# A two-layer hybrid decoder trunk: identity products on TensorE in front of nine of its waits

## The chip, the core and the metric

The kernel runs on one core of one Trainium2 chip. Each run gives one time, the device microseconds from launch to end. The profile is one execution of its own, with a span from the first to the last instruction. TensorE is called PE in the profile; its weight loads are a lane of their own (PEld), VectorE is DVE, ScalarE is ACT, GpSimd is POOL and SyncE is SP.

## The reference

Input x is 512 tokens by 1024 features, float32. Two layers, each with two residual steps, and a last norm:

```
for layer in (0, 1):
    hn = rms_norm(h, norm_mix_g[layer])
    proj = hn @ w_in[layer]                 # 1024 -> 2560, ten slices of 256
    y = concat(rg_lru(...)*gelu, hgrn2(...), multiscale_pool(...), sb*conv(sc*sx))
    h = h + y @ w_out[layer]                # 1024 -> 1024
    hn = rms_norm(h, norm_ffn_g[layer])
    if layer == 0: h = h + (silu(hn @ w_gate) * (hn @ w_up)) @ w_down        # 2816 wide
    else:          h = h + moe_swiglu(hn, w_router, w1, w3, w2)              # top 2 of 8, 3584 wide
out = rms_norm(h, final_norm_g)
```

The hgrn2 mixer is a gated linear recurrence, computed in chunks; the router takes two experts a token, and an expert computes `(silu(x @ w1[e]) * (x @ w3[e])) @ w2[e]` for its tokens.

## The kernel before

All engines run from hand-written queues: each engine's program is a list of instructions in the order of the code, and semaphores (`wait_ge`, `then_inc`) hold them apart. There is no scheduler; TensorE does what stands next in its list or waits for it.

**Precision.** Most matrix products are written as three fp32r products, `mm3` (lines 567 to 570): every operand is split into a high part and a rest, and hi*hi, hi*lo and lo*hi are added in PSUM. The splitting of weights is ScalarE's (`w_hi`) and VectorE's (`w_lo`) work. A second sort of product is plain float32: the levels of the hgrn2 scores (L629), the gates (L639), the pool product (L646), state updates (L688, L699, L704), the fold of the router's logits (L785), the rank counts (L789 to L793) and the picking of token rows (L968). A third sort is the transpose by the identity tile `idt`, also float32 (L586, L677, L717, L819, L854). `idt` is a 128x128 float32 tile that is loaded once.

**Stages on TensorE.** Per layer: `norm_transposes(2*layer)` turns four row tiles of 128 tokens (8 transposes each) into PSUM banks; ten `project` calls, with `level` calls between them; `hgrn_tail(layer)`, which does the output projection in pieces as the mixers' results arrive; `norm_transposes(2*layer+1)`; then in layer 0 a loop of 11 dense chunks, and in layer 1 the router and a loop over expert items. Norms are numbered m = 0 to 3 in that order.

**The norms.** ScalarE squares a row tile and sums it, VectorE and ScalarE make the scale, VectorE writes the scaled row (L1314), and TensorE transposes it (L586). For norms 0 to 2 the rows go alternately to two buffers, `ex_63` and `ex_64`, so VectorE may write row 2 only when TensorE has transposed row 0, and row 3 only after row 1 (`if i >= 2 and m < 3: dve.wait_ge(tr_done, 4 * m + i - 1)` in `norm_row`, L1313). Norm 3 has four buffers and no such wait. After the fourth row ScalarE and VectorE copy the banks out (L1020, L1329), and the next products start. In norms 1 and 3 the transposes of row 0 into banks 4 to 7 also wait for `h_ready`: these banks hold the output projection until VectorE has added it to h (L1612).

**End of the input projection.** After level 7 (L629) TensorE waits at the head of `hgrn_tail` for `pl_read`, `y_lo` and `w_lo_done`: VectorE must have split the first two mixers' results (L1412). `sb_read` is counted up by VectorE where it reads the slice SB out of PSUM (L1521), some instructions before.

**Router.** `mm3` with the router's weights into bank 0; VectorE copies the logits (`logits_copied`), TensorE folds them (L785), VectorE computes the two best experts (`route_ready`), TensorE counts ranks (L789 to L793), VectorE makes a 0/1 matrix `pick` (`pick_ready`), TensorE multiplies the token rows with it (L968), which gives the first item's tokens turned; VectorE and ScalarE split them into `xt` (L1173, L1709, L1714), and the first expert products (L898, L900) wait for that, and for `items_ready`.

Of the kernel before, what the change touches and what calls it, by code (L numbers as in the profile page):

```python
# [29 lines left out]
P = 128  # L30
# [69 lines left out]
def build(nc, x, w_in, w_out, w_gate, w_up, w_down, w_router, w1, w3, w2, norm_rows, params, ident,  # L100
          masks, moe_const, zeros, out):
    ctx = ExitStack()
    with ctx:
# [11 lines left out]
        def sb(name, shape, dt=F32):  # L115
            t = at(name, shape, dt, base[0])
            base[0] += size(shape, dt)
            return t

        def sem(name):  # L120
            return ctx.enter_context(nc.semaphore(name))
# [6 lines left out]
        idt = sb("idt", [P, P])  # L128
# [38 lines left out]
        def rows_of(m, i):  # L167

            return rows[i if m == 3 else i % 2]
# [54 lines left out]
        ps = ctx.enter_context(nc.psum_tensor("ps", [P, 8, 512], F32))  # L224
# [34 lines left out]
        sb_read = sem("sb_read")  # L259
# [306 lines left out]
        def _(pe):  # L566
# [8 lines left out]
            def wlo(n, k=KT):  # L575
                return w_los[:, n % 3, :].rearrange("p (k n) -> p k n", k=k)

            def norm_transposes(m):
                for i in range(NT):
                    pe.wait_ge(rows_done, 4 * m + i + 1)  # L580
                    for k in range(KT):
                        if i == 0 and k >= 4 and m % 2:
                            pe.wait_ge(h_ready, 4 * (m // 2) + k - 3)
                        if i == 0 and k in (4, 6) and m == 2:
                            pe.wait_ge(down_added, 4 * DC + k // 2 + 1)
                        last = pe.transpose(ps[:, k, i * P:(i + 1) * P], rows_of(m, i)[:, k * P:(k + 1) * P],  # L586
                                            idt[:, :])
                    last.then_inc(tr_done, 1)
# [77 lines left out]

            def hgrn_tail(layer):
                first = layer * LAYER1 + N_IN
                pe.wait_ge(pl_read, 2 * (layer + 1))
                pe.wait_ge(y_lo, 4 * layer + 2)  # L670
                pe.wait_ge(w_lo_done, first + 1)
# [13 lines left out]
                for c in range(NT - 1):  # L685
                    for hd in range(NH):
# [3 lines left out]
                                         start=True, stop=True)  # L690
                last.then_inc(ds_done, 1)
                pool_product(layer, 0)
                for c in range(NT):
# [4 lines left out]
                    for hd in range(NH):  # L698
                        last = pe.matmul(o_of(hd, c), scores[:, hd, c, :], vals[:, c, hd * HD:(hd + 1) * HD],  # L699
                                         start=c == 0 and hd < 2, stop=False)  # L700
                    if c:
                        for hd in range(NH):
# [3 lines left out]
                                             stop=c == NT - 1 and hd >= 2)  # L706
# [55 lines left out]
            for layer in range(DEPTH):  # L762
                norm_transposes(2 * layer)
                for i in range(N_IN):
                    project(layer, i)
                    if i >= 2:
                        level(layer, i - 2)
                    if i == 5:
                        gates(layer)
                hgrn_tail(layer)  # L770
                norm_transposes(2 * layer + 1)
                if layer == 0:
                    with pe.Fori(0, DC) as c:
                        dense_chunk(c)
# [3 lines left out]
            for k in range(KT):  # L778
                pe.wait_ge(in_lo, 3 * KT + k + 1)
                last = mm3(ps[0:NE, 0, :], wr_hi[:, k, :], wr_lo[:, k, :], act_hi[:, k, :], act_lo[:, k, :],  # L780
                           k == 0, k == KT - 1)
            last.then_inc(logits_turned, 1)
            pe.wait_ge(logits_copied, 1)
            for tt in range(NT):
                last = pe.matmul(ps[:, 1, tt * NE:(tt + 1) * NE], fold[0:NE, tt * P:(tt + 1) * P],  # L785
                                 idt[0:NE, 0:NE], start=True, stop=True)
            last.then_inc(logits_done, 1)
            pe.wait_ge(route_ready, 1)
            pe.matmul(ps[:, 3, 0:NT * NE], mcon[:, MC_LOWER:MC_LOWER + P], rt[:, 8, :], start=True, stop=False)  # L789
            for j in range(1, NT):  # L790
                last = pe.matmul(ps[:, 3, j * NE:NT * NE], mcon[:, MC_ONES:MC_ONES + P], rt[:, 8, 0:(NT - j) * NE],
                                 start=False, stop=j == NT - 1)
# [131 lines left out]
            def item_turned(n):  # L924
# [37 lines left out]
                    last.then_inc(yt_tr, 1)  # L962
                pe.sem_inc(t_done, 2 * EC)

            pe.wait_ge(pick_ready, 1)
            for k in range(KT):
                for i in range(NT):
# [2 lines left out]
                if k in (5, KT - 1):  # L970
                    last.then_inc(xt_tr, 1)

            turned_next = pe.alloc_register("pe_turned_next")
            pe.wait_ge(items_ready, 1)
            n_items = pe.value_load(items[0:1, 32:33], min_val=2, max_val=MAX_ITEMS)
# [304 lines left out]
        def _(dve):  # L1280
# [109 lines left out]
            def level_operand(layer, lv):  # L1390
                half = 1 << (lv - 1)
                if lv >= 3:
                    dve.wait_ge(level_done, 4 * (layer * LEVELS + lv - 1))
                dve.wait_ge(exp_done, 7 * layer + lv)
                e_left, e_right = views(ex[lv % 2], half)
                x_left, x_right = views(xs[lv % 2], half)
                k_left, _ = views(keys, half)
                _, q_right = views(qf, half)
                dve.tensor_tensor(x_left, k_left, e_left, ALU.mult)
                dve.tensor_tensor(x_right, q_right, e_right, ALU.mult).then_inc(xs_ready, 1)  # L1400
# [641 lines left out]
```

## Time and profile before

| | |
|---|---|
| time, three runs | 2129.79 us median (2128.96 to 2131.98) |
| the profiled execution | 2134.22 us, of which the span 2132.6 us |
| PE busy | 2012.5 us, 94% of the span |
| PEld / DVE / ACT / POOL busy | 84% / 73% / 52% / 5% |
| chain that ended last | PE 78%, DVE 11%, ACT 5%, issue 5% |
| mean granted TensorE clock | 0.976 of full speed |

How to read it: the granted clock has two levels here, 1.00 (2.4 GHz) and 0.50 (1.2 GHz), and the mean of a window says how much of it was spent at either. A matmul's time in the timeline is from its start to a modelled end; matmuls overlap, so the pace is read from a run of them: (time of the run less one matmul) by (count less one), or window by count. In a timeline row "[7.00 <-issue]" is the time that the engine stood idle before the row and what ended it; "issue" is a wait whose releaser the profile doesn't name. The start of a merged row is that of its first instruction; x32 is the number of instructions in it.

### The profile page before, as it was taken

The numbers are of one execution on the slowest core, as the hardware profiler recorded it, in microseconds if no ns is written. First come the engines' busy times: TensorE is split into PE (matmuls) and PEld (weight loads), VectorE is DVE, ScalarE is ACT, GpSimd is POOL, SyncE is SP. The second block draws the span as 40 slices with busy tenths as digits, with TensorE's granted clock in tenths as the row PEclk, the third lists the DMA queues.
The fourth block names the chain that finished last, engine by engine and source line by source line (L and its number), as shares of the span: only waits on it lengthen the run. The fifth ranks groups of instructions, "written<-read, shape, count | busy, mean of one in ns | idle before, by whom it ended". The sixth has DMA issues, their size and how long they took to land.

```text
span 2132.6 us, 33531 instructions
## 1 busy us (share of the span) xinstructions
PE 2012.5 (94%) x12158; PEld 1782.0 (84%) x12159; DVE 1549.3 (73%) x1622; ACT 1109.5 (52%) x1272; POOL 113.1 (5%) x105
## 2 busy tenths in 40 slices
PE   7998999999989988899999999999999999999993
PEld 6777878778778777899999988788999888999782
DVE  6766553443557484788878889899788898888896
ACT  5532433233335423455555577777555776555773
POOL 0000000000000000300010020200100201000202
PEclk9999999999999999899999999999999999999997
DMA  5311732323322121777677789999777899777983
GB/s 189 104 55 50 257 100 78 118 77 100 98 79 79 60 69 67 245 256 256 234 256 258 258 304 378 345 379 359 264 252 257 301 374 332 245 246 258 352 329 140
DMA packets 218795, 450.95 MB, mean 211 GB/s; under 512 B 13073, under 2 KB 64289, under 8 KB 218753
## 3 DMA queue, kind: packets, MB, share of 16 engines
q1 hardware_dynamic: 210256, 420.53, 56.7%
q0 software_dynamic: 8496, 29.85, 3.8%
q8 instruction: 28, 0.46, 0.1%
q14 instruction: 15, 0.11, 0.0%
HBM read 432.50 MB, written 17.84 MB: 211 GB/s over the span
## 4 chain that ended last, share of the span: by engine, by line
PE 78%; DVE 11%; ACT 5%; issue 5%; DMA 1%; POOL 0%; DVEq 0%; ACTq 0%; SPq 0%; POOLq 0%
PE ps L568 16%; PE ps L570 16%; PE ps L569 16%; PE ps L898 12%; PE ps L915 8%; PE ps L900 5%; PE ps L917 3%; DVE w_lo L1703 2%; DVE w_lo L1291 1%; ACT w_hi L998 1%; ACT w_hi L1149 1%; ACT w_hi L1151 1%; PE ps L629 1%; DMA raw<-in_w_in_dram 1%; DVE scores L1408 1%
## 5 line engine op out<-in xcount | busy, mean ns | idle before, releaser
L1703 DVE TENSOR_TENSOR w_lo<-raw,w_hi 128x2048 fp32r<-128x2048 f32 x340 | 768.7, 2285 | 136.5 <-ACT w_hi L1151 134.3
L898 PE MATMUL ps<-xt,w_hi 128*128 128x320 f32 x1792 | 465.3, 347 | 3.9 <-DVE xt L1714 3.6
L900 PE MATMUL ps<-xt,w_lo 128*128 128x160 f32 x1792 | 424.2, 237 | 0.0
L1149 ACT ACTIVATE w_hi<-raw 128x1024 fp32r<-128x1024 f32 x340 | 357.3, 1051 | 118.9 <-PE ps L900 62.1
L1151 ACT ACTIVATE w_hi<-raw 128x1024 fp32r<-128x1024 f32 x340 | 356.3, 1048 | 0.0
L900 PEld LDWEIGHTS ps<-xt,w_lo 128*128 128x128 f32 x1792 | 343.1, 191 | 0.1
L898 PEld LDWEIGHTS ps<-xt,w_hi 128*128 128x128 f32 x1792 | 337.2, 188 | 4.5 <-issue 4.4
L568 PE MATMUL ps<-act_hi,w_hi 128*128 128x512 f32 x608 | 244.3, 402 | 14.4 <-DVE act_lo L1329 7.2
L915 PE MATMUL ps<-ht,w_hi 128*128 128x320 f32 x896 | 235.9, 348 | 8.5 <-DVE gated L1823 8.5
L569 PE MATMUL ps<-act_lo,w_hi 128*128 128x512 f32 x608 | 242.5, 399 | 0.0
L570 PE MATMUL ps<-act_hi,w_lo 128*128 128x512 f32 x608 | 242.2, 398 | 0.0
L917 PE MATMUL ps<-ht,w_lo 128*128 128x160 f32 x896 | 212.1, 237 | 0.0
L568 PE MATMUL ps<-w_hi,xt 128*128 128x512 f32 x448 | 177.6, 397 | 0.7 <-issue 0.7
L570 PE MATMUL ps<-w_hi,xt 128*128 128x512 f32 x448 | 178.0, 397 | 0.0
L569 PE MATMUL ps<-w_lo,xt 128*128 128x512 f32 x448 | 177.1, 395 | 0.0
L915 PEld LDWEIGHTS ps<-ht,w_hi 128*128 128x128 f32 x896 | 168.1, 188 | 10.7 <-DVE gated L1823 5.7
L917 PEld LDWEIGHTS ps<-ht,w_lo 128*128 128x128 f32 x896 | 171.1, 191 | 0.0
L568 PEld LDWEIGHTS ps<-act_hi,w_hi 128*128 128x128 f32 x608 | 116.2, 191 | 44.8 <-issue 12.3
L1638 DVE TENSOR_TENSOR hid_d<-silu_d,ps 128x512 f32<-128x512 f32 x22 | 15.1, 688 | 172.3 <-PE ps L570 172.3
L570 PEld LDWEIGHTS ps<-act_hi,w_lo 128*128 128x128 f32 x608 | 116.1, 191 | 27.5
L569 PEld LDWEIGHTS ps<-act_lo,w_hi 128*128 128x128 f32 x608 | 116.2, 191 | 26.7
L568 PE MATMUL ps<-w_hi,act_hi 128*128 128x256 f32 x384 | 112.4, 293 | 18.4 <-issue 14.0
(322 smaller groups left out, 3104.8 us busy)
## 6 DMA issues: line engine op xcount, KB each, us to landing
raw<-in_moe_w_dram SPq DMA_DIRECT2D x672, 512.0 KB, 5.1
raw<-in_w_in_dram SPq DMA_DIRECT2D x20, 1024.0 KB, 5.1
raw<-in_ffn_w_gate_dram SPq DMA_DIRECT2D x11, 1024.0 KB, 5.4
raw<-in_ffn_w_up_dram SPq DMA_DIRECT2D x11, 1024.0 KB, 5.4
raw<-in_ffn_w_down_dram SPq DMA_DIRECT2D x11, 1024.0 KB, 4.8
raw<-in_w_out_dram SPq DMA_DIRECT2D x8, 1024.0 KB, 4.9
y_rows<-mult POOLq DMA_DIRECT2D x1, 8192.0 KB, 25.6
y_rows<-yacc POOLq DMA_DIRECT2D x8, 512.0 KB, 5.2
```

The costliest lines, as they stand in the source:

```text
L568: pe.matmul(o_, lhi, rhi, start=start, stop=False)
L569: pe.matmul(o_, lhi, rlo, start=False, stop=False)
L570: return pe.matmul(o_, llo, rhi, start=False, stop=stop)
L629: last = pe.matmul(ps[:, 4 + 2 * ct + half, c * P:(c + 1) * P], a, b, start=True, stop=True)
L898: pe.matmul(pairs_of(ps[:, bank, 0:2 * NW]), hi_[:, k % 4, f * P:(f + 1) * P], xt[:, k, :, 0:NW], start=k == 0, stop=False)
L900: last = pe.matmul(ps[:, bank, NW:2 * NW], lo_[:, k % 4, f * P:(f + 1) * P], xt[:, k, 0, 0:NW], start=False, stop=k == KT - 1)
L915: pe.matmul(pairs_of(ps[:, bank, 0:2 * NW]), hi_[:, f % 2, d * P:(d + 1) * P], ht_n[:, f, :, :], start=f == 0, stop=False)
L917: last = pe.matmul(ps[:, bank, NW:2 * NW], lo_[:, f % 2, d * P:(d + 1) * P], ht_n[:, f, 0, :], start=False, stop=f == 3)
L998: act.activation(w_his[:, n % 3, :], raw[:, n % 3, :], ACT.Copy).then_inc(w_hi_done, 1)
L1149: act.activation(slot_hi[p % 6][:, 0:half], raw6(p)[:, 0:half], ACT.Copy)
L1151: act.activation(slot_hi[p % 6][:, half:PIECE], raw6(p)[:, half:PIECE], ACT.Copy).then_inc(w_hi_done, 1)
L1703: dve.tensor_tensor(slot_lo[p % 6], raw6(p), f32(slot_hi[p % 6]), ALU.subtract) \
```

## The change

A helper `spin(o_, n)` issues n products of the identity tile with itself, float32, 128x128 by 128x128, into a part of PSUM that nothing reads. It is called with fixed counts at seven places of the code, which nine times run in a launch:

| place | count | stands in front of |
|---|---|---|
| head of `hgrn_tail`, both layers | 55, 55 | `pl_read`, `y_lo`, `w_lo_done` |
| norms 1 and 3, row 0, before k = 6 | 26, 26 | `h_ready` |
| norm 2, before row 0 | 28 | `rows_done` |
| after the router's logits | 6 | `logits_copied` |
| after the fold | 26 | `route_ready` |
| after the rank counts | 14 | `pick_ready` |
| after the picking | 28 | `items_ready`, then `xt_lo_done` |

That is 264 products. In `hgrn_tail` a wait for `sb_read` is new as well, since bank 0 holds a slice that VectorE reads. No other line is changed.

```
+            def spin(o_, n):
+                for _ in range(n):
+                    pe.matmul(o_, idt[:, :], idt[:, :], start=True, stop=True)
+
             def norm_transposes(m):
                 for i in range(NT):
+                    if m == 2 and i == 0:
+                        spin(ps[:, 0, 0:P], 28)
                     pe.wait_ge(rows_done, 4 * m + i + 1)
                     for k in range(KT):
+                        if i == 0 and k == 6 and m % 2:
+                            spin(ps[:, 0, P:2 * P], 26)
...
             def hgrn_tail(layer):
                 first = layer * LAYER1 + N_IN
+                pe.wait_ge(sb_read, 2 * (layer + 1))
+                spin(ps[:, 0, 0:P], 55)
                 pe.wait_ge(pl_read, 2 * (layer + 1))
                 pe.wait_ge(y_lo, 4 * layer + 2)
...
             last.then_inc(logits_turned, 1)
+            spin(ps[:, 7, 0:P], 6)
             pe.wait_ge(logits_copied, 1)
...
             last.then_inc(logits_done, 1)
+            spin(ps[:, 7, 0:P], 26)
             pe.wait_ge(route_ready, 1)
...
+            spin(ps[:, 7, 0:P], 14)
             pe.wait_ge(pick_ready, 1)
...
+            spin(ps[:, 7, 0:P], 28)
             turned_next = pe.alloc_register("pe_turned_next")
             pe.wait_ge(items_ready, 1)
```

The order of TensorE's list at the head of `hgrn_tail` in layer 0, before (L629 is the last level, L568 to L570 the output projection; the brackets name the semaphores waited for):

```order
L570 MATMUL ps<-act_hi,w_lo 128x512
L629 MATMUL ps<-xs_66 128x128 [waits level_read,xs_ready]
L629 MATMUL ps<-xs_66 128x128 x7
L629 MATMUL ps<-xs_66 128x128 [waits level_read]
L629 MATMUL ps<-xs_66 128x128 x7
L568 MATMUL ps<-w_hi,act_hi 128x256 [waits w_lo_done,y_lo,pl_read]
```

The same place now (the line numbers are those of the changed file; L637 is L629 of before, L580 the identity product):

```order
L637 MATMUL ps<-xs_66 128x128 [waits level_read,xs_ready]
L637 MATMUL ps<-xs_66 128x128 x7
L637 MATMUL ps<-xs_66 128x128 [waits level_read]
L637 MATMUL ps<-xs_66 128x128 x7
L580 MATMUL ps<-idt 128x128 [waits sb_read]
L580 MATMUL ps<-idt 128x128 x54
L568 MATMUL ps<-w_hi,act_hi 128x256 [waits w_lo_done,y_lo,pl_read]
```

The 55 products stand between the last level and the wait that the output projection had; nothing else moved. The list counts a product as the program writes it: the level is 16 of them here.

The router on TensorE, before (L785 is the fold, L789 to L793 the rank counts, L968 the picking):

```order
L785 MATMUL ps<-idt,fold 128x8 [waits logits_copied]
L785 MATMUL ps<-idt,fold 128x8 x3
L789 MATMUL ps<-rt,mcon 128x32 [waits route_ready]
L791 MATMUL ps<-rt,mcon 128x24
L791 MATMUL ps<-rt,mcon 128x16
L791 MATMUL ps<-rt,mcon 128x8
L793 MATMUL ps<-rt,mcon 128x32
L968 MATMUL ps<-pick,ex_63 128x160 [waits pick_ready]
```

And now:

```order
L580 MATMUL ps<-idt 128x128 x6
L796 MATMUL ps<-idt,fold 128x8 [waits logits_copied]
L796 MATMUL ps<-idt,fold 128x8 x3
L580 MATMUL ps<-idt 128x128 x26
L801 MATMUL ps<-rt,mcon 128x32 [waits route_ready]
L803 MATMUL ps<-rt,mcon 128x24
L803 MATMUL ps<-rt,mcon 128x16
L803 MATMUL ps<-rt,mcon 128x8
L805 MATMUL ps<-rt,mcon 128x32
L580 MATMUL ps<-idt 128x128 x14
L981 MATMUL ps<-pick,ex_63 128x160 [waits pick_ready]
```

Three of the blocks stand each ahead of one small group of real products; a block is issued whole before the semaphore behind it is looked at.

## Rows read from the trace of the kernel before

**Rows 1.** Waits of TensorE: engine, tile, line, waited for: us in total, times, longest.

```profile
PE ps L568 <- issue: 14.7, 5, 7.0
PE ps L586 <- DVE ex L1314: 14.3, 4, 10.1
```

**Rows 2.** Windows: us; busy (count) of PE, PEld, DVE, ACT, POOL; clock, DMA, GB/s.

```profile
172.16:176.57 4.41, 4.41 (x20) 4.41 (x21) 4.38 (x6) 0.00 (x0) 0.00 (x0) 0.50 0.00 0
777.85:780.73 2.88, 2.88 (x13) 2.88 (x14) 2.88 (x5) 0.00 (x0) 0.00 (x0) 0.50 0.00 0
238.01:244.84 6.83, 6.27 (x26) 5.10 (x26) 3.75 (x8) 2.60 (x6) 0.55 (x1) 0.50 0.98 392
838.72:844.66 5.94, 4.31 (x34) 3.36 (x32) 4.13 (x9) 2.48 (x6) 3.58 (x6) 1.00 0.66 208
860.53:866.02 5.49, 5.49 (x21) 5.49 (x21) 4.95 (x18) 0.00 (x0) 2.37 (x1) 0.50 0.75 280
866.02:871.75 5.73, 5.73 (x43) 5.73 (x43) 4.87 (x20) 0.97 (x1) 4.37 (x5) 1.00 0.59 186
876.30:879.72 3.42, 3.42 (x17) 3.42 (x16) 2.64 (x4) 3.39 (x4) 0.28 (x1) 0.50 0.49 162
210.00:230.00 20.00, 20.00 (x169) 20.00 (x168) 9.61 (x8) 5.75 (x3) 0.00 (x0) 1.00 0.40 126
```

**Rows 3.** Groups by form, TensorE, 852 to 873 us: one line.

```profile
L968 PE MATMUL ps<-pick,ex 128*128 128x160 f32 x32 | 7.5, 369 | 1.5 <-DVE pick L1725 1.5
```

**Rows 4.** Timeline, TensorE, end of the input projection, both layers: start us, us, [idle].

```profile
163.11 2.06 PE L629 MATMUL ps<-xs 64*128 64x128 f32 x32
172.16 0.55 PE L568 MATMUL ps<-w_hi,act_hi 128*128 128x256 f32 x1 [7.00 <-issue]
...
777.85 0.55 PE L568 MATMUL ps<-w_hi,act_hi 128*128 128x256 f32 x1 [6.99 <-issue]
```

**Rows 5.** Timeline, VectorE, beside the same place in layer 0.

```profile
157.55 1.29 DVE L1521 TENSOR_TENSOR scv<-ps,scv 128x512 f32<-128x512 f32 x2
...
187.31 0.35 DVE L1565 COPY state<-ps 128x64 f32<-128x64 f32 x2 [3.25 <-PE ps L688]
```

**Rows 6.** Timeline, TensorE, norm 1 (layer 0, second norm).

```profile
234.15 0.82 PE L586 MATMUL ps<-idt,ex 128*128 128x128 f32 x6
238.10 2.78 PE L586 MATMUL ps<-idt,ex 128*128 128x128 f32 x10 [3.13 <-DVE h L1612]
241.23 3.76 PE L586 MATMUL ps<-idt,ex 128*128 128x128 f32 x16 [0.35 <-DVE ex L1314]
```

**Rows 7.** Timeline, VectorE, rows 2 and 3 of norm 1.

```profile
239.89 1.29 DVE L1314 SCALAR_TENSOR_TENSOR ex<-h,small,xs 128x1024 f32<-128x1024 f32 x1
...
241.70 1.28 DVE L1314 SCALAR_TENSOR_TENSOR ex<-h,small,xs 128x1024 f32<-128x1024 f32 x1
```

**Rows 8.** Timeline, TensorE, norm 2 (layer 1, first norm).

```profile
620.09 4.72 PE L586 MATMUL ps<-idt,ex 128*128 128x128 f32 x24 [3.13 <-DVE ex L1314]
625.53 1.09 PE L586 MATMUL ps<-idt,ex 128*128 128x128 f32 x8 [0.72 <-DVE ex L1314]
```

**Rows 9.** Timeline, VectorE, row 2 of norm 2.

```profile
622.38 1.28 DVE L1314 SCALAR_TENSOR_TENSOR ex<-h,small,xs 128x1024 f32<-128x1024 f32 x1
```

**Rows 10.** Timeline, TensorE, norm 3 (layer 1, second norm).

```profile
838.72 2.14 PE L586 MATMUL ps<-idt,ex 128*128 128x128 f32 x16
...
843.57 1.09 PE L586 MATMUL ps<-idt,keys 128*128 128x128 f32 x8 [0.72 <-DVE keys L1314]
```

**Rows 11.** Timeline, TensorE, router and start of the expert items.

```profile
852.66 1.05 PE L785 MATMUL ps<-idt,fold 8*128 8x8 f32 x8 [0.77 <-DVE fold L1664]
856.68 0.64 PE L789 MATMUL ps<-rt,mcon 128*128 128x32 f32 x2 [2.97 <-DVE rt L1693]
...
860.53 1.43 PE L968 MATMUL ps<-pick,ex 128*128 128x160 f32 x4 [1.50 <-DVE pick L1725]
...
875.75 0.41 PE L898 MATMUL ps<-xt,w_hi 128*128 128x320 f32 x1 [3.56 <-DVE xt L1714]
```

More of the change, by code:

```diff
@@ L576, in wlo, with spin @@
                 return w_los[:, n % 3, :].rearrange("p (k n) -> p k n", k=k)
+            def spin(o_, n):
+                for _ in range(n):
+                    pe.matmul(o_, idt[:, :], idt[:, :], start=True, stop=True)
             def norm_transposes(m):
                 for i in range(NT):
+                    if m == 2 and i == 0:
+                        spin(ps[:, 0, 0:P], 28)
                     pe.wait_ge(rows_done, 4 * m + i + 1)
                     for k in range(KT):
+                        if i == 0 and k == 6 and m % 2:
+                            spin(ps[:, 0, P:2 * P], 26)
                         if i == 0 and k >= 4 and m % 2:
@@ L668, in hgrn_tail @@
                 first = layer * LAYER1 + N_IN
+                pe.wait_ge(sb_read, 2 * (layer + 1))
+                spin(ps[:, 0, 0:P], 55)
                 pe.wait_ge(pl_read, 2 * (layer + 1))
@@ L782, in _ @@
             last.then_inc(logits_turned, 1)
+            spin(ps[:, 7, 0:P], 6)
             pe.wait_ge(logits_copied, 1)
@@ L787, in _ @@
             last.then_inc(logits_done, 1)
+            spin(ps[:, 7, 0:P], 26)
             pe.wait_ge(route_ready, 1)
@@ L963, in item_turned @@
                 pe.sem_inc(t_done, 2 * EC)
+            spin(ps[:, 7, 0:P], 14)
             pe.wait_ge(pick_ready, 1)
@@ L971, in _ @@
                     last.then_inc(xt_tr, 1)
+            spin(ps[:, 7, 0:P], 28)
             turned_next = pe.alloc_register("pe_turned_next")
```

## The prediction, written before the changed kernel ran

> **What bounds the kernel now.** I read the page first: TensorE is busy for 94% of the span and stands for 78% of the chain that ended last, so whatever moves TensorE's list moves the end, unless another engine is ahead at that place. Then its waits [rows 1]. The longest entry, "issue", 14.7 us in 5 waits with a longest of 7.0, is mostly the two waits at the head of the output projection [rows 4]. Then the granted clock window by window [rows 2]: it is at one of two levels, and falls to 0.50 (1.2 GHz) after TensorE has stood still, and the first real work after a long wait then runs at that level: 4.41 us in layer 0, 2.88 us in layer 1, 3.42 us at the first expert products. That is what identity products in the waits can give back. What they can cost is in the same rows: a block is issued whole, in order, and if it takes longer than the wait the real work behind it is late.
>
> **The price of one identity product.** It is plain float32, 128 columns. The nearest rows are those of the picking, plain float32 too. The program has 32 such products (8 k by 4 row tiles). The trace has 64 instructions: x32 for the buffer `ex` alone, and as many for the other two [rows 3]. The fold is 4 products in the program's list and x8 in the trace [rows 11]; the last level is 16 and x32 [rows 4]. Transposes are one for one: 8 a row tile, x8 [rows 8]. The block isn't transposes but products, so each becomes two instructions. Their pace: 43 instructions of 160 columns in 5.73 us at full clock, 0.133 us each, and 21 in 5.49 us, 0.261, at half [rows 2]. By columns 128 take 0.133 x 128/160 = 0.107. Six transposes of 128 columns took 0.82 us, 0.137 each with the tail of the last one in it [rows 6]. I take 0.11 for an instruction and 0.22 us for a product, bounds 0.21 and 0.27; below both lies the case that a product is one instruction, a rival below. So 55 take 12.1 us, 28 take 6.2, 26 take 5.7, 14 take 3.1 and 6 take 1.3; all 264 take 58 us.
>
> A page of the Trainium skill, "TensorE: Matmul & The Clock Gate" (Back-to-back issue gap), gives 55.6 ns for a product of 128 columns at full clock. By that figure 55 products would be 3.1 us and every block would fit into its wait. Its page "FP8 and Floating Point Precision" (TensorE Precision Notes) says that true FP32 makes four passes through the array. This case's trace agrees with the four passes, with 0.133 us for each of two instructions of 160 columns.
>
> **How much half a clock costs.** At full clock 169 instructions of 256 columns run in 20 us, 0.118 each; at half, 20 in 4.41 us [rows 2], 0.22 counted with one that reaches over the edge, 0.21 without. So a stretch at half clock would take 0.56 of its time at full, and gives back 0.44. I take it that the clock holds over a block: the picking's products are float32 like the block's, and during them the clock rose from 0.50 to 1.00 [rows 2].
>
> **Head of the output projection, layer 0.** The last level ends at 163.11 + 2.06 = 165.17 [rows 4], its last instruction is streamed some 0.16 us earlier, so the block starts at 165.0; the new wait for `sb_read` costs nothing, VectorE's reading was over at 158.84 [rows 5]. 165.0 + 12.1 = 177.1, where the real work began at 172.16: 4.9 us late. Back comes 0.44 x 4.41 = 1.9. Net +3.0. Nobody hides this: the output pieces, the state products and the pool product follow on TensorE, and VectorE stood idle for 3.25 us until the state products were there [rows 5].
>
> **The same place, layer 1.** The wait was 6.99 us [rows 4], so 4.9 us late again; cold work 2.88 us, back 1.3. Net +3.6.
>
> **Norm 1 (26 products between k = 5 and k = 6 of row 0).** The block starts at 234.8 and ends at 240.5, where k = 6 began at 238.10 [rows 6]. Row 0 is then turned at 240.9. VectorE's row 2 shares the buffer and waits for it: 241.0 for 239.89, 1.1 us late, and row 3 stands 1.81 us behind row 2 [rows 7]. The last 8 transposes took from about 243.05 to 244.99 at half clock; now they start 1.1 us later and take 1.1 instead of 1.95. Net +0.2.
>
> **Norm 2 (28 before row 0).** The wait began at 620.09 - 3.13 = 616.96 [rows 8]; block from 616.8 to 623.0, 2.9 us late. Row 0 is turned at 624.05, so VectorE's row 2 starts at 624.1 for 622.38 [rows 9], and rows 2, 3 and all behind it move by that. The last transposes were at full clock already (8 in 1.09 us [rows 8]). Net +1.7.
>
> **Norm 3 (26 inside row 0).** No wait stood here: 16 transposes run through from 838.72 [rows 10], and the clock was 1.00 through the whole norm [rows 2]. Block from 839.4 to 845.1, 26 transposes at 0.11 behind it and 0.16 of tail, end at 848.1. Before: 843.57 + 1.09 = 844.66. The pauses of the norm swallow the rest. Net +3.4, the purest loss, and the router waits for it.
>
> **Router.** 6 products: 0.4 us late at the fold (their end 853.05 for 852.66). 26 behind the fold: end near 859.65, where the rank counts began at 856.68; the counts, 10 instructions, then take 1.3 us instead of 2.35 to 859.03 (860.53 - 1.50) [rows 11], end 860.95. 14: to 863.9, where the picking began at 860.53. It takes 64 x 0.133 = 8.5 us throughout instead of 5.5 at half clock and the rest at full, end 872.4. 28: to 878.6, where the first expert product began at 875.75 [rows 11]. So 2.85 late, less 0.44 x 3.42 = 1.5 of cold expert products [rows 2]. Net +1.35. VectorE's list up to `items_ready` moves by about 2 us and stays hidden behind the last block.
>
> **Sum.** 3.0 + 3.6 + 0.2 + 1.7 + 3.4 + 1.35 = 13.2 us. The profiled execution took 2134.2 us, so 2147.4 for one like it. The median of the runs lies 4.4 us lower, at 2129.8, and I put the sum on that: 2143.0 us. The 264 products are nearly all exposed in their last part, so 0.01 us a product is 2.6 us of sum: with 0.21 it is 10.6, with 0.27 about 26.
>
> **Rivals.**
>
> *One instruction a product (faster).* If the block's products cost 0.11 us like transposes, 55 take 6.0 and end at 171.0, inside the wait; 28 take 3.1 and just fit in norm 2 (wait 3.13) and before the experts (3.56), 26 take 2.9 and fit behind the fold (2.97). Then only gains are left: 1.9 + 1.3, 0.9 in norm 1, in the router 1.1 on the counts and 1.5 on the experts, less 0.5 in norm 3 where there is no wait. Sum -6.2, 2123.6 us. For it: each count times 0.11 is about its wait [rows 1, 4, 8, 11]. Against it: every float32 product in the trace stands there twice. It decides from about 0.15 us a product downwards, where gains and delays balance. 8%.
>
> *The delays are absorbed at the output projection.* If VectorE or ScalarE set the pace there, the 3.0 and 3.6 drop out: 2136.4 us. Against it the 3.25 us for which VectorE waited for TensorE [rows 5]. 5%.
>
> *The clock falls all the same.* Then the 1.9 + 1.3 + 1.5 us aren't given back, nor the 2.8 us of the picking and the 1.1 of the counts, and blocks themselves run partly at half clock: 2152 us and up. A weaker form concerns the norms. The page "TensorE: Matmul & The Clock Gate" (Part 4: PE-mode transpose) says that transposes don't count as activity as other products do. By it the clock would fall in norms 2 and 3 behind the block. In the trace the clock did stay at 0.50 through 26 transposes of norm 1, but it stayed at 1.00 through all of norm 3 [rows 2]. Two stretches of 3.4 us at half clock would be 3 us more: 2146. 4% for the strong form; the weak one lies in the range.
>
> *The blocks do nothing measurable*, being shorter than waits and the clock unmoved: 2129.8 us, 3%.
>
> **How the numbers follow.** My forecast has 80%, with a range of its own of 2139 to 2148: lower by a cheaper product and by absorbed parts, higher by 0.23 to 0.24 us a product or a colder norm. The range for 8 in 10 is 2135 to 2150: it leaves out the 8% and 3% below, and above it most of the strong clock case and prices near 0.27, whose row has the tail of the last instruction in it. A change under 0.2% (4.3 us) can't be told from none here. Slower by more: the forecast's whole share, the absorbed case and the clock case, 88%. Within: 4%. Faster: 8%.
>
> **What would show it.** The trace of the changed kernel should have 528 instructions of the identity product, at 0.11 us each; the first L568 behind the levels should start about 12.1 us after the last level ends, in both layers; the clock should be 1.00 from there on, and through the picking; norm 3 should last 9.4 us from its first transpose instead of 5.9; VectorE's row 2 of norm 2 should wait for TensorE. I am wrong if there are 264 instructions, if the wait behind a block is not zero, or if TensorE has a new wait behind the output pieces that shows the delay absorbed.

## The result, and the profile after

| | before | after |
|---|---|---|
| time, six runs each | 2131.82 us (2128.96 to 2134.51) | 2153.33 us (2145.87 to 2154.8) |
| ratio of the runs, 95% interval | | 1.0095 [1.0078, 1.0112] |
| the profiled execution | 2134.22 us, span 2132.6 | 2153.51 us, span 2151.8 |
| mean granted clock | 0.976 | 0.985 |

The change makes the kernel slower. The medians lie 21.5 us apart, the two spans 19.2 us. The difference of 2.3 us is that the profiled execution of before was a long one, 2.4 us over the median of its runs, and that of after was not. The forecast was 2143.0 us: the direction was right, the size was not.

The granted clock is higher than before, so the products do what they are made for. TensorE's part of the chain that ended last went up from 78% to 84%, and the products' own line stands in it with 3%:

```profile
core 0: 2151.8 us, clock 0.985
PE 84%; DVE 7%; ACT 4%; issue 3%; DMA 1%; POOL 0%; ACTq 0%; DVEq 0%; SPq 0%; POOLq 0%
```

**The products themselves.** The profile's entry for their line (duration in ns: min/median/max):

```profile
L580 PE MATMUL ps<-idt x528: 270/275/377, 163.7 to 891.5; 128*128 128x128 f32 x176
```

264 products are 528 instructions. The time of one, 275 ns, isn't its pace, since they overlap. The pace is in the timeline of TensorE, at the head of the output projection in both layers, which answers to [rows 4]:

```profile
161.71 2.06 PE L637 MATMUL ps<-xs 64*128 64x128 f32 x32
163.70 12.55 PE L580 MATMUL ps<-idt 128*128 128x128 f32 x110
176.00 0.36 PE L568 MATMUL ps<-w_hi,act_hi 128*128 128x256 f32 x1
...
774.64 12.55 PE L580 MATMUL ps<-idt 128*128 128x128 f32 x110
786.95 0.36 PE L568 MATMUL ps<-w_hi,act_hi 128*128 128x256 f32 x1
```

(12.55 - 0.28) / 109 = 0.1126 us an instruction, 0.225 a product. The wait of 7.0 us is gone, and the first real product comes 14.29 us after the level's start where it came 9.05 after it. It is now at full clock, 0.36 us for 0.55.

**Norms.** TensorE in norms 1, 2 and 3, as in [rows 6, 8, 10]:

```profile
236.42 5.97 PE L580 MATMUL ps<-idt 128*128 128x128 f32 x52
242.22 1.26 PE L594 MATMUL ps<-idt,ex 128*128 128x128 f32 x10
...
618.95 6.41 PE L580 MATMUL ps<-idt 128*128 128x128 f32 x56
625.20 1.91 PE L594 MATMUL ps<-idt,ex 128*128 128x128 f32 x16
...
847.36 5.97 PE L580 MATMUL ps<-idt 128*128 128x128 f32 x52
853.17 1.25 PE L594 MATMUL ps<-idt,ex 128*128 128x128 f32 x10
```

The transposes behind the block follow at once, with no idle time before them. In norm 2 the delay goes through VectorE, whose row 2 now waits for TensorE [rows 9], and so do the state products' readers at the head of layer 0 [rows 5]:

```profile
626.34 1.28 DVE L1328 SCALAR_TENSOR_TENSOR ex<-h,small,xs 128x1024 f32<-128x1024 f32 x1 [1.84 <-PE ps L594]
```

```profile
189.18 0.35 DVE L1579 COPY state<-ps 128x64 f32<-128x64 f32 x2 [6.50 <-PE ps L698]
```

**Router**, as in [rows 11]:

```profile
864.65 1.05 PE L796 MATMUL ps<-idt,fold 8*128 8x8 f32 x8
865.63 6.07 PE L580 MATMUL ps<-idt 128*128 128x128 f32 x52
871.54 0.31 PE L801 MATMUL ps<-rt,mcon 128*128 128x32 f32 x2
...
872.58 3.37 PE L580 MATMUL ps<-idt 128*128 128x128 f32 x28
875.78 0.71 PE L981 MATMUL ps<-pick,ex 128*128 128x160 f32 x4
...
884.48 5.05 PE L580 MATMUL ps<-idt 128*128 128x128 f32 x41
889.89 1.93 PE L580 MATMUL ps<-idt 128*128 128x128 f32 x15 [0.36 <-issue]
891.85 0.41 PE L910 MATMUL ps<-xt,w_hi 128*128 128x320 f32 x1
```

Every wait of this stretch is filled, and the picking runs at full clock (a window: us, busy and count of PE, PEld, DVE, ACT, POOL, then clock, DMA, GB/s):

```profile
875.70:884.40 8.70, 8.70 (x67) 8.70 (x66) 7.80 (x29) 0.97 (x1) 5.80 (x5) 1.00 0.46 154
```

But the last block isn't one piece: its first 41 instructions span 5.05 us instead of the 4.8 that 0.113 gives, then TensorE stands for 0.36 us. From start to start there are two long steps in it, 0.42 us and 0.65 us, together 0.84 us over the usual pace, and nothing is waited for.

**A place where nothing was changed.** The waits of TensorE have an entry that before didn't have, and the timeline shows where it is, behind the transposes that end the first expert item:

```profile
PE ps L910 <- issue: 3.3, 1, 3.3
```

```profile
1072.40 0.27 PE L973 MATMUL ps<-idt,yturned 128*32 128x128 f32 x1
1075.98 0.49 PE L910 MATMUL ps<-xt,w_hi 128*128 128x320 f32 x1 [3.31 <-issue]
```

The code behind the transposes is the end of a pass through the loop over the items:

```
with pe.Fori(0, n_items) as n:                  # L977 before, L991 after
    with pe.If(pe.snap(turned_next, ...) > 0):  # L978 before, L992 after
        item_turned(n)
    with pe.Else():
        item_one(n)
```

TensorE's queue, a row kind of its own (PEldq), has branches under both lines. Those of the `If` are 12: eight are its tests, one an item, and four are the jump from the end of `item_turned` over the code of `item_one`. Here they are, before and after, in ns min/median/max, each followed by the loop's own branch:

```profile
L978 PEldq COMPARE_BRANCH  x12: 84/169/305, 872.4 to 1974.3; - x12
L977 PEldq COMPARE_BRANCH  x8: 82/213/229, 1057.8 to 2094.7; - x8
```

```profile
L992 PEldq COMPARE_BRANCH  x12: 84/169/3345, 891.5 to 1993.3; - x12
L991 PEldq COMPARE_BRANCH  x8: 82/213/243, 1075.2 to 2113.7; - x8
```

Eleven of the twelve are as before. The slow one starts at 1071.75, is the second of the twelve in time and the first of the four jumps: it takes 3.3 us for 0.3. The other three jumps take 0.17 us in both kernels, and the loop's own branch, which follows at 1075.24, is as fast as before. So what is slow is the jump over `item_one`, the first time it is taken. Then the clock falls, as it did behind the 7 us waits of before (windows: us, busy and count of PE, PEld, DVE, ACT, POOL, clock):

```profile
1072.67:1075.90 3.23, 0.00 (x0) 0.00 (x0) 1.05 (x1) 2.44 (x4) 0.92 (x2) 1.00 0.27 76
1076.15:1079.56 3.41, 3.41 (x15) 3.41 (x16) 1.72 (x1) 3.41 (x4) 0.00 (x0) 0.50 1.01 364
```

**Where the 19.2 us are.** The two traces hold the same real products in the same order, so each can be found in both, and the difference of its start times is the shift at that point. How much the shift grows over a stretch:

| stretch (times of before) | forecast | measured |
|---|---|---|
| up to the end of the last level, layer 0 | 0 | -1.40 |
| head of the output projection, layer 0 (to 196.6) | +3.0 | +3.28 |
| norm 1 (234.2 to 246.5) | +0.2 | +0.36 |
| norm 2 (616.6 to 628.1) | +1.7 | +1.82 |
| head of the output projection, layer 1 (770.6 to 801.6) | +3.6 | +3.96 |
| norm 3 (838.7 to 846.2) | +3.4 | +3.52 |
| router up to the first experts (846.2 to 911.4) | +1.35 | +3.02 |
| end of the first expert item (911.4 to 1092.6) | 0 | +4.52 |
| all other stretches together | 0 | +0.1 |
| sum | +13.2 | +19.2 |

### The profile page after: what moved, and what is told of

It is laid out like the page before. It is cut to its first block, busy times and chain, and to the rows that moved or that the text cites. A ratio compares the mean times of both kernels' runs of the same rounds, so it can differ in the third digit from the quotient of the medians.

```text
span 2151.8 us, 34587 instructions
## 1 busy us (share of the span) xinstructions
PE 2057.4 (96%) x12686; PEld 1829.1 (85%) x12687; DVE 1550.2 (72%) x1622; ACT 1109.5 (52%) x1272; POOL 110.2 (5%) x105
## 4 chain that ended last, share of the span: by engine, by line
PE 84%; DVE 7%; ACT 4%; issue 3%; DMA 1%; POOL 0%; ACTq 0%; DVEq 0%; SPq 0%; POOLq 0%
PE ps L568 17%; PE ps L570 17%; PE ps L569 17%; PE ps L910 12%; PE ps L927 7%; PE ps L912 5%; PE ps L929 3%; PE ps L580 3%; DVE w_lo L1717 2%; PE ps L637 1%; DVE w_lo L1305 1%; ACT w_hi L1163 1%; ACT w_hi L1165 1%; ACT w_hi L1012 1%; DMA raw<-in_w_in_dram 1%
## 5 line engine op out<-in xcount | busy, mean ns | idle before, releaser
L1717 DVE TENSOR_TENSOR w_lo<-raw,w_hi 128x2048 fp32r<-128x2048 f32 x340 | 769.1, 2286 | 136.1 <-ACT w_hi L1165 133.9
L568 PE MATMUL ps<-act_hi,w_hi 128*128 128x512 f32 x608 | 244.2, 402 | 14.1 <-ACT win L1038 7.2
L570 PE MATMUL ps<-act_hi,w_lo 128*128 128x512 f32 x608 | 242.8, 399 | 0.0
L568 PE MATMUL ps<-w_hi,xt 128*128 128x512 f32 x448 | 177.7, 397 | 0.7 <-issue 0.7
L570 PE MATMUL ps<-w_hi,xt 128*128 128x512 f32 x448 | 177.9, 397 | 0.0
L927 PEld LDWEIGHTS ps<-ht,w_hi 128*128 128x128 f32 x896 | 168.1, 188 | 10.8 <-DVE gated L1837 5.7
L568 PEld LDWEIGHTS ps<-act_hi,w_hi 128*128 128x128 f32 x608 | 116.3, 191 | 44.4 <-issue 12.2
L570 PEld LDWEIGHTS ps<-act_hi,w_lo 128*128 128x128 f32 x608 | 116.3, 191 | 27.5
L1305 DVE TENSOR_TENSOR w_lo<-raw,w_hi 128x2048 fp32r<-128x2048 f32 x28 | 64.1, 2292 | 81.5 <-ACT w_hi L1012 80.8
```

The lines of the kernel that those rows point to most:

```text
L568: pe.matmul(o_, lhi, rhi, start=start, stop=False)
L570: return pe.matmul(o_, llo, rhi, start=False, stop=stop)
L927: pe.matmul(pairs_of(ps[:, bank, 0:2 * NW]), hi_[:, f % 2, d * P:(d + 1) * P], ht_n[:, f, :, :], start=f == 0, stop=False)
L1305: dve.tensor_tensor(w_los[:, n % 3, :], raw[:, n % 3, :], f32(w_his[:, n % 3, :]), ALU.subtract) \
L1717: dve.tensor_tensor(slot_lo[p % 6], raw6(p), f32(slot_hi[p % 6]), ALU.subtract) \
```

## The experiments

All times are medians in us, beside runs of before that were made with them. "Place" is the number of instructions that a kernel adds to TensorE's list, modulo 256: 4 for a product (two weight loads, two products), 2 for a transpose. The instruction counts of the traces agree (33,531 before, 34,587 after: 1056 more, for 264 products).

| run | products | place | time | before | ratio, interval | slowest of the 12 branches of the `If`, ns |
|---|---|---|---|---|---|---|
| before | 0 | 0 | 2131.82 | | | 305 |
| after | 264 | 32 | 2153.33 | 2131.82 | 1.0095 [1.0078, 1.0112] | 3345 |
| before, 32 empty instructions | 0 | 0 | 2133.0 | 2132.58 | 1.0 [0.9991, 1.0009] | as before |
| after, 224 empty instructions | 264 | 32 | 2152.47 | 2132.58 | 1.0092 [1.0077, 1.0108] | 3665 |
| about half | 116 | 208 | 2123.25 | 2132.58 | 0.996 [0.9947, 0.9974] | 403 |
| transposes | 264 | 16 | 2130.1 | 2132.58 | 0.9989 [0.998, 0.9998] | 3365 |
| before + 8 | 8 | 32 | 2138.33 | 2132.45 | 1.0026 [1.0011, 1.0041] | 3445 |
| after - 8 | 256 | 0 | 2140.55 | 2132.45 | 1.0045 [1.0032, 1.0059] | 320 |
| fitted, 128 | 128 | 0 | 2123.68 | 2132.45 | 0.9958 [0.9945, 0.9972] | 305 |
| fitted, 136 | 136 | 32 | 2130.21 | 2132.45 | 0.9989 [0.998, 0.9998] | 3805 |
| heads alone | 110 | 184 | 2139.02 | 2132.15 | 1.003 [1.0018, 1.0041] | 403 |
| norms 1 and 2 alone | 54 | 216 | 2135.22 | 2132.15 | 1.0014 [1.0005, 1.0024] | 305 |
| norm 3 alone | 26 | 104 | 2142.98 | 2132.15 | 1.0049 [1.0032, 1.0066] | 3490 |
| router alone | 74 | 40 | 2143.24 | 2132.15 | 1.0047 [1.003, 1.0064] | 3365 |
| norm 3 + 38 in the heads | 64 | 0 | 2135.86 | 2132.26 | 1.0017 [1.0008, 1.0026] | 305 |
| router + 54 in the heads | 128 | 0 | 2130.04 | 2132.26 | 0.9988 [0.9979, 0.9998] | 305 |

A kernel's branches were seen in its one profiled execution. Other executions have only their times, and some single ones lie far from the rest: one of six of after is 7.5 us under its median, one of six of before + 8 is 6.7 us under it, and one of seven of the heads alone, whose jump was fast, 5.4. Whether the jump is slow or fast in every execution of a kernel isn't shown; the two kernels that were traced twice were the same both times.

Two theories were tried for the 4.5 us at the jump (the texts on record call it the branch at the end of the first item). P: it depends on where the code behind the products stands in the blocks in which TensorE's instructions are fetched. The profile has instruction packets as a queue of its own:

```profile
q8 instruction: 33, 0.54, 0.1%
```

33 packets hold 0.54 MB, 16,384 bytes each. Before had 28, and the kernels with 256, 512 and 1024 instructions more have 29, 30 and 32: a packet for each 256. L: it depends on how late or early the router and the expert items are against other engines.

**1. Empty instructions.** In before and in after:

```
+            for _ in range(32):            # 224 in after
+                pe.nop(nofuse=True)
             pe.wait_ge(const_loaded, 16)
```

> The kernel before with 32 empty instructions (nop) at the head of TensorE's list, in its first wait of 10 us; no identity products. It puts all of TensorE's code where it stands in the changed kernel within a 16 KB block of instructions (the change adds 1056 instructions of 64 bytes, four blocks of 256 and 32). Theory P (place of the code): the branch at the end of the first expert item, 0.3 us before and 3.3 us after, depends on where the loop's code lies, so it takes about 3.3 us here too, the clock falls behind it, and the time is some 4.5 us over before: about 2136. Theory L (lateness): the branch is slow since the items start 14 us later against the transfers; then it takes 0.3 us here and the time is that of before, 2132.

> The changed kernel with 224 empty instructions at the head of TensorE's list, in its first wait: all code stands within the 16 KB blocks as in the kernel before. Theory P: the branch at the end of the first item takes 0.3 us, and the time is about 4.5 us under the changed kernel, some 2148.5; the 0.9 us that the last block of 28 lost may go too. Theory L: nothing changes, 2153. If 224 empty instructions don't fit into 10 us, both are later by what sticks out, seen at the first transpose.

Neither moved the code: the counts of instructions and of fetch packets in both traces are those of the kernels without them, so they didn't reach the program that ran. The two are repeats of before and after, and say only that the medians repeat (2133.0 for 2132.6, 2152.5 for 2153.3) and that the slow jump is there again (3665 ns). Inconclusive on P and L.

**2. About half of the products, each block fitted to its wait.**

```
-                        spin(ps[:, 0, 0:P], 28)
+                        spin(ps[:, 0, 0:P], 13)
-                            spin(ps[:, 0, P:2 * P], 26)
+                            spin(ps[:, 0, P:2 * P], 13 if m == 1 else 0)
-                spin(ps[:, 0, 0:P], 55)
+                spin(ps[:, 0, 0:P], 27)
...                                          # router 3, 12, 6, 15; 48 nops at the head
```

> The changed kernel with blocks that fit their waits at 0.226 us a product: 27 at the head of the output projection (6.1 us of 7.0), 13 in norm 1, none in norm 3, 13 in norm 2, 3, 12, 6 and 15 in the router; and 48 empty instructions at the start, so that the code stands within its blocks as before. Theory S (the blocks were too long, the clock is what they give back): 1.9 + 1.3 at the two heads, 0.9 in norm 1, 1.1 on the rank counts, 1.5 on the first expert products: 6 to 7 us under before, about 2125. Rival N (a clock held over the waits is worth nothing since other engines set the pace behind them): within 1.5 us of before.

2123.25 us: 9.3 us (0.4%) under before, 30 us under after. Keeping the clock up pays where the block ends before the wait does. The 48 empty instructions left no trace here either (33,995 instructions, 464 more than before for 116 products), so the place is 208 and not the 0 that was meant.

**3. All 264, as transposes of the identity.**

```
-                    pe.matmul(o_, idt[:, :], idt[:, :], start=True, stop=True)
+                    pe.transpose(o_, idt[:, :], idt[:, :])
```

> The changed kernel with the same counts, but each product of the identity written as a transpose of the identity, which is one instruction. This makes the forecast's rival of one instruction a product real. Theory S: 0.11 us each, 55 end inside the wait, and if transposes hold the clock the sum is -6 us against before, about 2126, or 2130 with the slow branch. Rival T (transposes don't hold the clock): the clock falls in the waits as before, the transposes behind that take 0.21 us, and the real work is late and cold: 2135 to 2142.

A transpose is one instruction, so each block takes half the time. At the head of layer 0 the block of 55 ends before the wait does, and the clock is held (timeline, then a window):

```profile
164.00 6.22 PE L580 MATMUL ps<-idt 128*128 128x128 f32 x55
171.07 0.36 PE L568 MATMUL ps<-w_hi,act_hi 128*128 128x256 f32 x1 [0.85 <-issue]
```

```profile
167.00:177.00 10.00, 9.15 (x80) 8.94 (x79) 9.86 (x12) 2.60 (x2) 0.00 (x0) 1.00 0.01 2
```

But its jump is slow, 3365 ns, and its shift grows by 6.0 us between 911.4 and 1092.6. Without that it would be at 2124, an estimate, beside the run with about half. Its expert items start within a microsecond of that run's, and the one jump takes 0.4 us, the other 3.4: against L, as far as lateness at the items' start goes.

**4. Eight products more, eight fewer.** Before with 8 products (1.8 us) in layer 0's wait of 7.0 us; after with 18 instead of 26 in norm 1:

```
+                if layer == 0:
+                    pe.wait_ge(sb_read, 2 * (layer + 1))
+                    spin(ps[:, 0, 0:P], 8)
```

```
-                            spin(ps[:, 0, P:2 * P], 26)
+                            spin(ps[:, 0, P:2 * P], 18 if m == 1 else 26)
```

> The kernel before with one block of 8 identity products at the head of the output projection of layer 0 alone, 1.8 us in a wait of 7.0: it can't be late, and 5 us of the wait stay, so that the clock falls as before. But the 32 instructions put all later code of TensorE where it stands in the changed kernel, within blocks of 256 instructions. Theory P (place of the code): the branch at the end of the first item takes 3.3 us instead of 0.3, the clock falls behind it, time 4.5 us over before, about 2137. Theory L (another reason, such as the items' start): branch 0.3 us, time within 1.5 us of before, 2132.5.

> The changed kernel with 18 products instead of 26 in norm 1, where they cost next to nothing (0.4 us in all). Its 256 products are four whole blocks of instructions, so the later code stands as in the kernel before. Theory P: branch 0.3 us, time 4.5 to 5.5 us under the changed kernel, some 2148. Theory L: at most 1 us under it, 2152.

The clearest pair. Eight products in a wait that hides them four times over cost before 5.9 us, and taking eight away gives after back 12.8 us. The branches of the `If`, before with 8 and after less 8:

```profile
L993 PEldq COMPARE_BRANCH  x12: 83/169/3445, 872.3 to 1977.5; - x12
```

```profile
L992 PEldq COMPARE_BRANCH  x12: 80/169/320, 884.9 to 1979.0; - x12
```

In the traces the shift of the first grows by 5.7 us over the first item's end (3.1 in the jump, 2.6 behind it), that of the second by -0.1. This also settles L: the items of before with 8 start at 872.3 as in before (872.4), and the jump is slow; those of after less 8 start 12.5 us later, and it is fast.

P had forecast 4.5 us for the first run and 4.5 to 5.5 for the second, so most of the 12.8 is something else. The two traces put them together: 4.6 at the jump and behind it, 1.2 in norm 1, 1.2 in the router's last block, and the rest, 5.7, for the most part in single intervals of 3.41 us at half clock that after has and this run hasn't; such an interval costs about 1.5 us, and they come and go between executions of one kernel too.

**5. Blocks fitted to the waits, at place 0 and at place 32.** 27, 27, 16, 13, 0, 3, 12, 8, 22 products, in the order head layer 0, head layer 1, norms 1 to 3, router; and 29, 29, 18, 13, 0, 3, 13, 9, 22.

> Blocks that fit their waits, a little nearer to the waits' ends than in the halved version: 27 and 27 at the heads, 16 in norm 1, 13 in norm 2, none in norm 3, 3, 12, 8 and 22 in the router, 128 in all (two whole blocks of instructions: code as before). Theory S (what fits costs nothing and saves the cold work): as the halved version or 1 to 2 us better, 2121 to 2124. Theory P: the branch takes 0.3 us.

> As c1 with 8 products more, all in waits that have room (29 and 29 at the heads, 18 in norm 1, 13 behind the fold, 9 before the picking), which moves later code by 32 instructions. Theory P: branch 3.3 us and 4 to 5 us over c1, about 2127. Theory L: as c1 within 1 us.

Eight products more, nearly all hidden, 6.5 us slower, where P had said 4 to 5. The shifts differ by 5.7 us over the first item's end, 3.5 of it in the jump. The blocks of the faster one end just before the waits do:

```profile
165.87 6.29 PE L580 MATMUL ps<-idt 128*128 128x128 f32 x54
172.94 0.36 PE L568 MATMUL ps<-w_hi,act_hi 128*128 128x256 f32 x1 [0.78 <-issue]
```

**6. One group of blocks at a time.** All other counts are 0, and the wait for `sb_read` stands only where the heads have their blocks:

> The kernel before with the two blocks of 55 at the head of the output projection alone. By the forecast's sum 3.0 + 3.6 = +6.6 us, about 2139. If the two delays were absorbed, 2132.5. At half the price (no delay, clock kept) 2129. The code shifts by 440 instructions, a place that hasn't been tried: a slow branch would add 4.5 and is read in the trace.

> The kernel before with the blocks of norm 1 (26) and norm 2 (28) alone: forecast 0.2 + 1.7 = +1.9 us, about 2134.5. If VectorE did not wait for the transposes of row 0, norm 2 would cost nothing and the sum is 0. A slow branch would add 4.5 (read in the trace).

> The kernel before with the block of 26 in norm 3 alone, where no wait stood: forecast +3.4 us from the first transpose to the router's first product, about 2136. Rival: the pauses of the norm's last rows swallow more, +1 to +2. A slow branch would add 4.5 (read in the trace).

> The kernel before with the router's four blocks alone (6, 26, 14, 28): forecast +1.35 us; in the trace of the changed kernel they came to 3.0, of which 0.9 were a halt within the last block beside a fetch of instructions of 3.2 us. If the halt belongs to the router's transfers it comes here too: +2.5 to +3, 2135.5. If it belonged to the place of the code (here 40 instructions off, changed kernel 32), the same. The slow branch would add 4.5, which by theory P it should (40 is near 16 and 32, which were slow): 2140.

The heads alone cost 6.9 us (forecast 6.6), norms 1 and 2 alone 3.1 us, interval 1.1 to 5.1 (forecast 1.9). Norm 3 alone costs 10.8 and the router alone 11.1, far more than 3.4 and 1.35. In the trace with norm 3 alone the shift grows by 3.52 us over the norm, as in after, and by 5.70 at the jump, which stood at a slow place (104). That is 9.2 of the 10.8 us; the rest isn't placed. The branches, and the first product behind the jump:

```profile
L990 PEldq COMPARE_BRANCH  x12: 81/169/3490, 874.3 to 1980.3; - x12
```

```profile
1063.44 0.63 PE L908 MATMUL ps<-xt,w_hi 128*128 128x320 f32 x1 [3.44 <-issue]
```

The router alone: 3.0 us up to the experts as in after, 5.9 at the jump, 9.0 of 11.1.

**7. The same two, with the code put back.** Norm 3 alone and router alone, each with so many hidden products in the two 7 us waits that the added instructions are 256 and 512.

```
+                spin(ps[:, 0, 0:P], 19)     # norm 3's 26 kept; 27 with the router's 74
```

> The kernel before with 26 products inside row 0 of norm 3, as in the run with norm 3 alone, and 19 products in each of the two waits at the head of the output projection, where they fit (4.3 us in a wait of 7.0). The 38 further products make the added instructions 256, so the code behind them stands where it stands in the kernel before. Theory P (the place of the code in blocks of 256 instructions makes a branch slow): the branch at the end of the first expert item takes 0.3 to 0.4 us instead of 3.5, no half clock follows it, and the time is 5.7 us under norm 3 alone (2143.0) by that, and 0 to 4 us more by cold work that the products at the heads avoid: 2133 to 2137. Rival (norm 3's block costs by itself what the run with it alone showed, over 10 us): only the heads' gain, 2139 to 2143, with the branch as slow as there.

> The kernel before with the router's four blocks (6, 26, 14, 28) as in the run with the router alone, and 27 products in each of the two waits at the head of the output projection, where they fit. 74 and 54 are 128 products, 512 instructions, so the code behind stands where it stands in the kernel before. Theory P: the branch at the end of the first expert item takes 0.3 to 0.4 us, the trace is later by about 3 us at the first expert products and by nothing at the branch, and the last block takes 6.3 us instead of 7.3; with the heads' gain of 2 to 4 us the time is 2131 to 2135. Rival (the router's blocks cost 11 us by themselves): 2139 to 2142, with the branch at 3.4 us.

More products, and less time: 2135.86 for 2142.98 and 2130.04 for 2143.24. The first lies in P's range, the second 1 us under it, and both are under the rival's. One part of P's text for the second missed: its last block took 7.3 us and not 6.3, and its shift grew by 4.2 us up to the experts, not 3. The branches of the first, and the first product behind the jump:

```profile
L992 PEldq COMPARE_BRANCH  x12: 84/169/305, 873.9 to 1975.9; - x12
```

```profile
1060.03 0.41 PE L910 MATMUL ps<-xt,w_hi 128*128 128x320 f32 x1 [0.28 <-issue]
```

Over norm 3 its shift grows by 3.52 us, as in the run with norm 3 alone, so the block itself costs what was forecast for it. Over the first item's end its shift grows by -0.1 for +5.7: that part was the code's place.

## Why the prediction was wrong

**What held.** A product is two instructions, at 0.225 us for 0.22. The blocks run in order, and the real work follows at once behind them. The delays at the two heads aren't absorbed. The clock is at 1.00 behind the blocks: 1.00 over the picking and the first experts, where [rows 2] had 0.50. Five of the six terms came out at 3.28, 0.36, 1.82, 3.96 and 3.52 us for 3.0, 0.2, 1.7, 3.6 and 3.4; they are a little higher mostly because the price was 2% over the 0.22. Norm 3 was to last 9.4 us from its first transpose: from 846.71 to 856.17, 9.46. By the rule of the Trainium skill that transposes don't count as activity ("TensorE: Matmul & The Clock Gate", Part 4: PE-mode transpose) norms 2 and 3 would have cooled; here the clock stayed at 1.00 until the last transpose of both, and through blocks that were transposes themselves (experiment 3). In norm 2 of before it even rose from 0.50 while TensorE ran nothing but transposes:

```profile
620.30:623.72 3.42, 3.42 (x17) 2.78 (x15) 3.02 (x6) 2.31 (x6) 0.00 (x0) 0.50 0.00 0
623.72:627.00 3.28, 2.18 (x17) 1.71 (x16) 1.45 (x3) 0.54 (x2) 0.00 (x0) 1.00 0.01 2
```

Right behind norm 2 of after, though, the products run at half clock for 3.41 us from 632.41, after pauses of 0.7 and 1.5 us; and so they do in the repeat of after, but not in before and in after less 8, which have the same transposes. That interval would fit the rule of the Trainium skill; the rest doesn't.

**The step that failed** is the sum itself, "3.0 + 3.6 + 0.2 + 1.7 + 3.4 + 1.35 = 13.2 us". It counted what the added instructions do where they run, and nothing for what they do to the code behind them. They moved it by 1056 instructions, to a place where the jump over `item_one` takes 3.3 us instead of 0.3 the first time and leaves the clock at half behind it: +4.52 us in this trace, with half clock for 3.41 us, and 5.7 to 6.2 in the six others with a slow jump, where half clock lasts 6.83. Without it the result would have been 2148.8, an estimate, inside the range given. That it is the place is shown: of 16 kernels (with the two repeats), those at 0, 184, 208 and 216 have a slowest branch of 0.3 to 0.4 us and a growth of -0.1 to +0.1 us there, those at 16, 32, 40 and 104 one of 3.3 to 3.8 us and a growth of 4.5 to 6.2; 8 products added or taken away switch it, in both directions; and norm 3's and the router's blocks lose it with 38 and 54 products more. That the place repeats every 256 instructions fits all ten kernels at 0 and 32, whose added instructions run from none to 1056. What the jump waits for isn't shown. No rival had this. "If the wait behind a block is not zero" looked at the right kind of evidence at the wrong place.

**The router's term** was too small: 3.02 for 1.35 us. 0.35 of it is that the picking began 3.75 us late for 3.4. The larger part is the last block, 7.34 us for 6.2, which has the two long steps of 0.84 us together. The same steps are in the run with the router alone and in the router with 54 at the heads (0.94 and 0.86 us), and not in after less 8 products, whose block of 56 instructions has no step over 0.2 us. In after a fetch packet of q8 that took 3.2 us, where most take about 1, ends at 889.0, within the first step (888.72 to 889.14). But in after less 8 one of 2.2 us also ends inside the block, and no step is there; and in the router alone, which has the steps, q8's packet in the block took 0.9 us. So a long packet of q8 isn't it, and the cause of these steps stays open.

**The base.** The sum was put on the median of three runs, 2129.8; the median of six is 2131.8. The profiled execution on which the rows rest took 2134.2.

Together: 2153.3 - 2143.0 = 10.3 us is 2.0 of base, 4.5 of the jump, 1.7 of the router, 1.0 of the five other terms, and 2.3 by which the medians lie further apart than the spans, less 1.3 in the other stretches without a term (the first of them -1.40: half clock in two intervals of 3.41 us where before had 6.83 twice).

**The rivals.** "One instruction a product" fell at once; as an experiment it gave 2130.1 us, or some 2124 without its slow jump, where the rival had said 2123.6. "Absorbed" fell by the 3.28 and 3.96 us. "The clock falls all the same" would have reached 2152 us, near the result, and is wrong all the same: no block of after is followed at once by half clock. A total that fits isn't evidence for its mechanism.

**The better version.** Blocks that end before their waits do or about with them, nothing in norm 3, and the code at a fast place: 2123.25 and 2123.68 us, 0.4% faster than before.

## What to carry to other kernels

Filler that keeps the clock up pays only as far as it ends inside the wait, so its length has to be worked out from the pace of the very instruction (a float32 product is two), and where there is no wait it is pure loss. And when instructions are added to or taken from a long unrolled list, look in the trace for the branches and jumps behind them: one of them may become slow by the code's place alone, and a few instructions more may undo it. An ablation moves the code as well, so single parts don't add up (6.9 + 3.1 + 10.8 + 11.1 = 31.9 us for 21.5) unless the place is kept.

## What the runs showed of the hardware

- A jump of TensorE's queue over the code of an `Else` takes 0.3 to 0.4 us or 3.3 to 3.8 us the first time, depending on where the code stands, and 0.17 us the three times after. In the slow case three instruction packets come one after the other before TensorE goes on: in after one of queue q8 at 1072.73 us (0.9 us) and two of q14 at 1073.78 and 1074.95 (0.5 and 0.8 us), and the next product starts at 1075.98. With a fast jump the same packets are fetched at about the same distance behind it while TensorE goes on working (before: 1058.29, 1059.59 and 1060.44). All seven traces with a slow jump have one more packet of q8, 5 to 7 us behind the first (after: 1079.08); none of the nine with a fast one has. Why TensorE has to wait in one case isn't shown, and only eight places were seen. A period of 256 instructions, as many as come with a packet of 16,384 bytes, fits all of them and isn't proven.
- The idle time of 3.3 us at a slow jump is followed by half clock for 3.41 us in after and for 6.83 us in the six other traces that have one.
- Transposes of the identity held the clock in the wait as float32 products do, at half the cost: 0.110 us each, 55 in 6.22 us, with the clock at 1.00 behind them.
- Empty instructions on TensorE left nothing in the trace, neither in its counts nor in its packets, so they can't be used to move code.
